# Gate and up projections of a decoder layer by Strassen's seven block products, on one core

## The chip, the core and the metric

One core of a Trainium2 chip runs the whole layer in one launch. The metric is device time in microseconds (us) of that core. TensorE (PE) multiplies, ScalarE (ACT) and VectorE (DVE) copy, split and add, GpSimd (POOL) does elementwise work too, and SyncE (SP) issues the loads.

## What is computed

The part that the change touches is the first half of the feed-forward block (512 tokens, width 1024, hidden width 2816):

```
h = rms_norm(x, ffn_norm[l])
g = jnp.einsum('bsd,df->bsf', h, w_gate[l])
u = jnp.einsum('bsd,df->bsf', h, w_up[l])
x = x + jnp.einsum('bsf,fd->bsd', jax.nn.silu(g) * u, w_down[l])
```

Ahead of it lie the attention part (two groups of heads, one input projection) and the output projection; both stay as they are.

## The kernel before

Every float32 operand of a product is split in two parts of a shorter type: a high part, which ACT copies (`ffn_hi`, L389 through `split_hi`), and a low part, which DVE gets as operand minus high part (`split_lo`, L723). `product` (L1075 to L1079) then issues three matmuls for each 128x128 tile of stationary operand: high by high, high by low, low by high.

Weights come in tiles of 128x1024 (512 KB): of the gate and the up matrix each tile holds 128 hidden columns over the whole width of 1024 (eight blocks of 128), and 22 + 22 such tiles stand in turn, gate, up, gate, up (`columns`). A ring of four slots holds the raw tile, its high and its low part. `hidden` takes one tile: 8 blocks times 3 matmuls with 512 tokens as moving operand (`H2`), into one bank of PSUM. The first four tiles are done in two passes of 256 tokens, since the last two of the four groups of 128 tokens are normed and transposed (`turn_h2`) between them. ACT takes silu of the gate bank (L667), DVE multiplies it with the up bank (`gate`, L1042), and the two split the result (L671, L1046). Then come 22 tiles of the down projection (`down`), each 24 matmuls of 512 columns, with hidden tokens as stationary operand.

All order is written by hand: each engine runs its own list, and semaphores join them. DVE has, at the entry of the stage, for each group of 128 tokens the residual add (L1011), the Newton steps of the norm (L704 to L716), the norm itself (`h_normed`, L1028) and the low part of the transposed activations (`h2_lo`, L1016). GpSimd has nothing to do after the attention part (L354 to L366 are its rotary products there, 512 elements in each of 128 partitions, both inputs in SBUF).

## Time and profile before

| what | value |
|---|---|
| time, median of 3 runs (lowest to highest) | 684.35 us (684.1 to 685.02) |
| span of the profiled execution | 685.7 us, 1.35 above the median of the runs |
| PE busy | 654.8 us, 95% of the span |
| DVE, ACT, POOL busy | 366.3, 247.9, 79.3 us |
| first matmul of gate and up | 314.94 us from the start |
| first matmul of the down projection | 559.16 us |
| last matmul | 682.12 us |

The records give no time of the profiled execution other than its span. Times in the rows count from the start of that span. The duration of a matmul in a row holds its passage through the array; successive matmuls overlap, so their pace is read from the starts.

### The profile page before, as it was taken

How to read it: one execution, taken by the hardware profiler on the slowest of the kernel's cores; microseconds unless marked ns; L12 is line 12 of the kernel's file. 1: busy time of each engine (PE TensorE's matmuls, PEld its weight loads, DVE VectorE, ACT ScalarE, POOL GpSimd, SP SyncE). 2: the span in 40 equal slices, each digit the busy share in tenths (PEclk: the TensorE clock that was granted, in tenths of full speed). 3: DMA queues.
4: the chain of work that ended last, by engine and by line, in shares of the span. 5: the costliest groups of instructions: out<-in, count | busy, mean ns of one | idle time of the engine just before them, and what ended most of it. 6: DMA issues, size and time to landing. Idle time of an engine off the chain costs nothing.

```text
span 685.7 us, 9568 instructions
## 1 busy us (share of the span) xinstructions
PE 654.8 (95%) x3220; PEld 533.4 (78%) x3220; DVE 366.3 (53%) x703; ACT 247.9 (36%) x458; POOL 79.3 (12%) x64
## 2 busy tenths in 40 slices
...
DMA packets 19944, 61.42 MB, mean 90 GB/s; under 512 B 3024, under 2 KB 3408, under 8 KB 19920
## 3 DMA queue, kind: packets, MB, share of 16 engines
...
q8 instruction: 15, 0.25, 0.2%
...
## 4 chain that ended last, share of the span: by engine, by line
PE 77%; DVE 14%; issue 4%; ACT 2%; DMA 1%; SPq 0%; DVEq 0%; ACTq 0%
PE ps L1077 24%; PE ps L1079 23%; PE ps L1078 23%; PE ps L1142 3%; DVE small L713 2%; PE ps L1157 2%; DVE small L716 1%; DVE small L788 1%; DVE small L714 1%; PE ps L1109 1%; DVE w_lo L723 1%; ACT probs L480 1%; DMA w_raw<-wt 1%; DVE probsT_lo L822 1%; PE ps L1117 1%
## 5 line engine op out<-in xcount | busy, mean ns | idle before, releaser
L1077 PE MATMUL ps<-h_parts,w_hi 128*128 128x512 f32 (+1 forms) x576 | 227.5, 395 | 3.0 <-DVE h_parts L859 2.8
L1079 PE MATMUL ps<-h_parts,w_lo 128*128 128x512 f32 (+1 forms) x576 | 220.8, 383 | 0.0
L1078 PE MATMUL ps<-h_parts,w_hi 128*128 128x512 f32 (+1 forms) x576 | 219.0, 380 | 0.0
L723 DVE TENSOR_TENSOR w_lo<-w_raw,w_hi 128x1024 fp32r<-128x1024 f32 x93 | 118.4, 1273 | 79.1 <-ACT w_hi L389 78.8
L1077 PEld LDWEIGHTS ps<-h_parts,w_hi 128*128 128x128 f32 x576 | 109.5, 190 | 26.0 <-issue 7.3
L389 ACT ACTIVATE w_hi<-w_raw 128x1024 fp32r<-128x1024 f32 x93 | 97.4, 1053 | 81.8 <-PE ps L1079 80.4
L1079 PEld LDWEIGHTS ps<-h_parts,w_lo 128*128 128x128 f32 x576 | 109.1, 189 | 22.6
L1078 PEld LDWEIGHTS ps<-h_parts,w_hi 128*128 128x128 f32 x576 | 109.5, 190 | 19.0
L1042 DVE TENSOR_TENSOR gated<-ps,silu_gate 128x512 f32<-128x512 f32 x22 | 15.2, 692 | 154.9 <-PE ps L1079 154.9
L1079 PE MATMUL ps<-w_hi,hidden_parts 128*128 128x512 f32 x176 | 69.3, 394 | 0.0
L1077 PE MATMUL ps<-w_hi,hidden_parts 128*128 128x512 f32 x176 | 69.3, 394 | 0.0
L1078 PE MATMUL ps<-w_lo,hidden_parts 128*128 128x512 f32 x176 | 69.3, 394 | 0.0
L480 ACT ACTIVATE probs<-ps,small 128x128 f32<-128x128 f32 (+3 forms) x64 | 39.0, 614 | 40.6 <-DVE small L791 40.5
L671 ACT ACTIVATE hidden_parts<-gated 128x512 f32 (+1 forms) x22 | 13.9, 633 | 100.3 <-DVE gated L1042 100.3
L1078 PEld LDWEIGHTS ps<-w_lo,hidden_parts 128*128 128x128 f32 x176 | 32.9, 187 | 8.2
L1079 PEld LDWEIGHTS ps<-w_hi,hidden_parts 128*128 128x128 f32 x176 | 32.9, 187 | 8.2
L1077 PEld LDWEIGHTS ps<-w_hi,hidden_parts 128*128 128x128 f32 x176 | 32.9, 187 | 8.1
L667 ACT ACTIVATE silu_gate<-ps 128x512 f32<-128x512 f32 x22 | 13.2, 598 | 64.8 <-PE ps L1079 64.8
L490 ACT ACTIVATE probsT_hi<-ps 128x128 fp32r<-128x128 f32 (+3 forms) x48 | 19.3, 439 | 26.4 <-PE ps L1157 26.0
L788 DVE TENSOR_REDUCE small<-ps 128x2 f32<-128x256 f32 (+3 forms) x32 | 26.4, 824 | 1.1
L362 POOL TENSOR_TENSOR q_roped<-q_gained,cos 128x512 f32<-128x512 f32 x8 | 11.0, 1372 | 127.1 <-ACT q_gained L429 127.1
L822 DVE TENSOR_TENSOR probsT_lo<-ps,probsT_hi 128x128 fp32r<-128x128 f32 (+3 forms) x48 | 21.5, 482 | 3.2 <-ACT probsT_hi L490 3.2
...
## 6 DMA issues: line engine op xcount, KB each, us to landing
w_raw<-wt SPq DMA_DIRECT2D x98, 512.0 KB, 3.4
residual<-x SPq DMA_DIRECT2D x4, 512.0 KB, 4.8
...
ffn_gain<-gain SPq DMA_DIRECT2D x1, 512.0 KB, 3.3
...
```

What stands on the lines that cost most here:

```text
L389: nc.scalar.activation(WH[:, slot], RAW[:, slot], ACT.Copy).then_inc(w_hi, 1)
L480: nc.scalar.activation(PR[qt % 2][:, a, 0:W], ps[:, 2 + a, 0:W], ACT.Exp, bias=NB[:, i:i + 1], scale=RQ[:, i:i + 1], accum_out=SUM[:, i:i ...
L490: nc.scalar.activation(PTH[:, a, 0:qt + 1, qt * P:(qt + 1) * P], ps[:, bank, 0:(qt + 1) * P].rearrange("p (k q) -> p k q", q=P), ACT.Copy) ...
L671: nc.scalar.activation(HID[:, f, 0], AC[:, par], ACT.Copy).then_inc(ah_s, 1)
L723: nc.vector.tensor_tensor(WL[:, slot], RAW[:, slot], WH[:, slot].bitcast(F32), ALU.subtract).then_inc(w_lo, 1)
L788: nc.vector.tensor_reduce(MX[:, i], ps[:, 2:4, 0:W], AX.X, ALU.max).then_inc(mx_s, 1)
L822: nc.vector.tensor_tensor(PTL[at], ps[:, bank, 0:(qt + 1) * P].rearrange("p (k q) -> p k q", q=P), PTH[at].bitcast(F32), ALU.subtract).the ...
L1042: nc.vector.tensor_tensor(AC[:, par], ps[:, 5 + 2 * par], SG[:, par], ALU.mult).then_inc(gated_s, 1)
L1077: nc.tensor.matmul(dst, lh, rh, start=start, stop=False, skip_group_check=True)
L1078: nc.tensor.matmul(dst, lh, rl, start=False, stop=False, skip_group_check=True)
L1079: return nc.tensor.matmul(dst, ll, rh, start=False, stop=stop, skip_group_check=True)
L1142: ins = nc.tensor.matmul(ps[:, 2 + a, 0:W], left[rows[a], qs], right[rows[a], 0:W], start=n == 0, stop=n == 2, skip_group_check=True)
```

## The change

The gate and up projections are cut in 11 units of 256 hidden columns (two tiles of gate, two of up). In a unit the activations are a 2x2 block matrix, first and second half of the tokens by first and second half of the width of 1024, and the weights are one too: first and second half of the width by gate (B11, B21) and up (B12, B22). Seven block products (Q1 to Q7, in Winograd's form) take the place of eight. One product is two tiles of 128 hidden columns times 4 blocks of the width times 3 matmuls: 24 matmuls with 256 tokens as moving operand. In the table of order `ORDER` a unit has seven of them, 77 in all.

- PE: `hidden` is replaced by `gate_product`. Q1, Q6, Q7 and Q4 of a unit add up in one bank, Q2, Q5 and Q3 in others; Q2 and the pair Q5/Q3 have one bank each for all units.
- GpSimd: `w_sum` makes four sums of raw weights per unit (128x1024 each): T1 = B11 + B12 (for Q5), T2 = T1 + B22 (Q6), B22 + B12 (Q7), T2 + B21 (Q4). In the first unit two sums of activations (`SR[:, 2]` and `SR[:, 3]`, also 128x1024) stand between them.
- ACT: a high part for each of the 77 products (`product_hi`), copies of the bank's partial sums (`keep_q1`, `keep_q16`, `keep_q167`), silu of both halves, and five high parts of activation sums (`sum_hi`). `product_hi(n)` waits for the product before the fourth slot came round: product n - 4.
- DVE: the 77 low parts (`product_lo`), two sums of activations in two pieces (`sums`), their five low parts (`sum_lo`), and per unit `gate_first`, `up_second`, `hidden_second` and the two operations of `up_and_hidden_first`.
- SP: loads of 512 KB as before, in another cut and into two rings of four slots; those of the second unit wait for the end of the output projection.
- The splitting of the hidden activations moves into the down stage (`hidden_hi`, `hidden_lo`), whose matmuls stay.

```diff
 LOADS_BEFORE = (RING3 // 3 + 1, RING3 // 3 + 1, RING3 // 3 + 1, 2)
 assert RING3 % 4 == 3
+def gate_order():
+    order = [(q, u) for q in ("Q1", "Q2") for u in (0,)] + [("Q1", 1), ("Q2", 1)]
+    order += [("Q6", 0), ("Q5", 0), ("Q7", 0), ("Q6", 1), ("Q4", 0), ("Q3", 0), ("Q7", 1), ("Q5", 1)]
+    for u in range(2, UNITS):
...
+            def w_sum(u, n):
+                b11, b21, b12, b22 = (unit_raw(u, role) for role in ROLES)
+                if n == 1:
+                    if u == 0:
+                        pool.wait_ge(wo_s, 2 * TT)
+                    else:
+                        pool.wait_ge(c_lo, PLACE["Q5", u - 1] + 1)
+                    unit_raw_wait(pool, u, "B11")
+                    unit_raw_wait(pool, u, "B12")
+                    nc.gpsimd.tensor_tensor(T1[:], b11, b12, ALU.add).then_inc(sums_w, 1)
+                if n == 2:
+                    if u >= 1:
+                        pool.wait_ge(c_lo, PLACE["Q6", u - 1] + 1)
+                    unit_raw_wait(pool, u, "B22")
+                    pool.wait_ge(sums_w, 4 * u + 1)
+                    nc.gpsimd.tensor_tensor(T2[:], T1[:], b22, ALU.add).then_inc(sums_w, 1)
+                if n == 3:
+                    pool.wait_ge(sums_w, 4 * u + 2)
+                    nc.gpsimd.tensor_tensor(b12, b22, b12, ALU.add).then_inc(sums_w, 1)
+                if n == 4:
+                    unit_raw_wait(pool, u, "B21")
+                    pool.wait_ge(c_lo, PLACE["Q2", u] + 1)
+                    pool.wait_ge(sums_w, 4 * u + 3)
+                    nc.gpsimd.tensor_tensor(b21, T2[:], b21, ALU.add).then_inc(sums_w, 1)
+            w_sum(0, 1)
+            w_sum(0, 2)
+            pool.wait_ge(h2r_s, TT)
+            nc.gpsimd.tensor_tensor(SR[:, 2], H2R[:, 0:KTH, 0:HALF], H2R[:, 0:KTH, HALF:SEQ], ALU.subtract).then_inc(ss3_s, 1)
+            w_sum(0, 3)
+            pool.wait_ge(ss2_s, 2)
+            nc.gpsimd.tensor_tensor(SR[:, 3], H2R[:, KTH:KT, 0:HALF], SR[:, 1], ALU.add).then_inc(ss4_s, 1)
+            w_sum(0, 4)
+            for u in range(1, UNITS):
+                for n in (1, 2, 3, 4):
+                    w_sum(u, n)
...
-            def ffn_hi(r, n):
-
-                if isinstance(r, int) and r == 0:
+            def product_hi(n):
+                if n < SLOTS:
                     act.wait_ge(wo_s, TT)
                 else:
-                    act.wait_ge(w_used, round_w_used(r - 1, n))
-                split_hi(n, r + (LOADS_BEFORE[n] + 1))
+                    act.wait_ge(c_used, n - SLOTS + 1)
+                if n >= PRODUCTS:
+                    down_raw_wait(act, n - PRODUCTS)
+                else:
+                    q, u = ORDER[n]
+                    if q in ("Q1", "Q2", "Q3"):
+                        unit_raw_wait(act, u, {"Q1": "B11", "Q2": "B21", "Q3": "B22"}[q])
+                    else:
+                        act.wait_ge(sums_w, 4 * u + {"Q5": 1, "Q6": 2, "Q7": 3, "Q4": 4}[q])
+                nc.scalar.activation(WH[:, n % SLOTS], product_source(n), ACT.Copy).then_inc(c_hi, 1)
...
+            sum_hi(0, SR[:, 1], ss2_s, 2)
+            sum_hi(1, SR[:, 0], sa_s, 2)
+            def keep_q1(u):
+                act.wait_ge(c_used, PLACE["Q1", u] + 1)
+                if u >= 1:
+                    act.wait_ge(g0_s, u)
+                nc.scalar.activation(C1[:], ps[:, bank("Q1", u)], ACT.Copy).then_inc(c1_s, 1)
...
+            def silu_first(u):
+                act.wait_ge(g0_s, u + 1)
+                nc.scalar.activation(G0[:], G0[:], ACT.Silu).then_inc(sg0_s, 1)
+            def silu_second(u):
+                act.wait_ge(c_used, PLACE["Q4", u] + 1)
+                if u >= 1:
+                    act.wait_ge(hid_s, 2 * u - 1)
+                nc.scalar.activation(G1[:], ps[:, bank("Q4", u)], ACT.Silu).then_inc(sg1_s, 1)
...
+            for n, (q, u) in enumerate(ORDER):
+                if q == "Q1":
+                    keep_q1(u)
+                if q == "Q6":
+                    keep_q16(u)
+                if q == "Q7":
+                    keep_q167(u)
+                if q == "Q4":
+                    silu_second(u)
+                if q == "Q3" and u + 1 < UNITS:
+                    silu_first(u + 1)
+                if (q, u) == ("Q2", 0):
+                    silu_first(0)
+                product_hi(n + 3)
+                if n == 1:
+                    sum_hi(2, SR[:, 2], ss3_s, 1)
+                    sum_hi(3, H2R[:, KTH:KT, HALF:SEQ], h2r_s, TT)
+                if n == 4:
+                    sum_hi(4, SR[:, 3], ss4_s, 1)
+                if n >= PRODUCTS - 2:
+                    hidden_hi(n - (PRODUCTS - 2))
+            for f in range(2, FT):
+                hidden_hi(f)
+                if f + 1 < FT:
+                    product_hi(PRODUCTS + f + 1)
...
-            def ffn_lo(r, n):
-                split_lo(n, r * 4 + (G_FFN + n + 1))
+            def product_lo(n):
+                dve.wait_ge(c_hi, n + 1)
+                nc.vector.tensor_tensor(WL[:, n % SLOTS], product_source(n), WH[:, n % SLOTS].bitcast(F32),
+                                        ALU.subtract).then_inc(c_lo, 1)
...
+            def sums(tt):
+                dve.wait_ge(h2r_s, tt + 1)
+                first, second = slice((tt - 2) * P, (tt - 1) * P), slice(tt * P, (tt + 1) * P)
+                nc.vector.tensor_tensor(SR[:, 0, :, first], H2R[:, 0:KTH, second], H2R[:, KTH:KT, second],
+                                        ALU.subtract).then_inc(sa_s, 1)
+                dve.wait_ge(sa_s, tt - 1)
+                nc.vector.tensor_tensor(SR[:, 1, :, first], SR[:, 0, :, first], H2R[:, 0:KTH, first],
+                                        ALU.subtract).then_inc(ss2_s, 1)
+            def sum_lo(i, source):
+                dve.wait_ge(sc_hi, i + 1)
+                nc.vector.tensor_tensor(SC[:, i, 1], source, SC[:, i, 0].bitcast(F32), ALU.subtract).then_inc(sc_lo, 1)
...
-                if tt >= 1:
-                    ffn_lo(0, tt - 1)
+                if tt in (1, 2):
+                    product_lo(tt - 1)
...
-                if tt >= 1:
-                    h2_lo(tt - 1)
-            ffn_lo(0, TT - 1)
-            h2_lo(TT - 1)
...
+                if tt in (1, 2):
+                    first_lo(tt - 1)
+            sums(2)
+            product_lo(2)
+            sums(3)
+            sum_lo(0, SR[:, 1])
+            sum_lo(1, SR[:, 0])
+            def gate_first(u):
+                dve.wait_ge(c1_s, u + 1)
+                dve.wait_ge(c_used, PLACE["Q2", u] + 1)
+                if u >= 1:
+                    dve.wait_ge(hid_s, 2 * u)
+                nc.vector.tensor_tensor(G0[:], ps[:, bank("Q2", u)], C1[:], ALU.add).then_inc(g0_s, 1)
...
+            def up_and_hidden_first(u):
+                dve.wait_ge(v2_s, u + 1)
+                dve.wait_ge(c_used, PLACE["Q3", u] + 1)
+                nc.vector.tensor_tensor(U0[:], ps[:, bank("Q3", u)], V2[u % 2][:], ALU.subtract).then_inc(u0_s, 1)
+                dve.wait_ge(sg0_s, u + 1)
+                dve.wait_ge(u0_s, u + 1)
+                nc.vector.tensor_tensor(HID[:, 2 * u:2 * u + 2, 0:HALF], G0[:].rearrange("p (f q) -> p f q", f=2),
+                                        U0[:].rearrange("p (f q) -> p f q", f=2), ALU.mult).then_inc(hid_s, 1)
...
+            for n, (q, u) in enumerate(ORDER):
+                if (q, u) == ("Q2", 0):
+                    gate_first(0)
+                if q == ("Q5" if u == 1 else "Q7"):
+                    up_second(u)
+                if q == "Q4":
+                    hidden_second(u)
+                if q == "Q3":
+                    up_and_hidden_first(u)
+                    if u + 1 < UNITS:
+                        gate_first(u + 1)
+                product_lo(n + 3)
+                if n == 1:
+                    sum_lo(2, SR[:, 2])
+                    sum_lo(3, H2R[:, KTH:KT, HALF:SEQ])
+                if n == 4:
+                    sum_lo(4, SR[:, 3])
+                if n >= PRODUCTS - 2:
+                    hidden_lo(n - (PRODUCTS - 2))
+            for f in range(2, FT):
+                hidden_lo(f)
+                if f + 1 < FT:
+                    product_lo(PRODUCTS + f + 1)
...
+            def gate_product(n):
+                q, u = ORDER[n]
                 if n == 0:
-                    turn_h2(2)
-                if n == 2:
-                    turn_h2(3)
-            pe.wait_ge(h2l, TT)
-            for f, j in ((0, 0), (0, 1), (1, 0), (1, 1)):
-                hidden(f, f, j, slice(SEQ // 2, SEQ))
-            with pe.Fori(1, GATE_ROUNDS) as r:
-                for par in range(2):
-                    hidden(r * 2 + par, par, 0, slice(0, SEQ))
-                    hidden(r * 2 + par, par, 1, slice(0, SEQ))
-
+                    pe.wait_ge(a1_lo, 2)
+                if u == 0 and q in ("Q6", "Q5", "Q7", "Q4", "Q3"):
+                    pe.wait_ge(sc_lo, {"Q6": 1, "Q5": 2, "Q7": 3, "Q4": 4, "Q3": 5}[q])
+                if q == "Q1":
+                    if u < 2:
+                        pe.wait_ge(res, TT + 2 * u + 1)
+                    else:
+                        pe.wait_ge(sg1_s, u - 1)
+                if q == "Q2":
+                    if u == 0:
+                        pe.wait_ge(res, TT + 2)
+                    else:
+                        pe.wait_ge(g0_s, u)
+                if q == "Q6":
+                    pe.wait_ge(c1_s, u + 1)
+                if q == "Q7":
+                    pe.wait_ge(v2_s, u + 1)
+                if q == "Q4":
+                    pe.wait_ge(v3_s, u + 1)
+                if q == "Q5" and u >= 1:
+                    pe.wait_ge(u0_s, u)
+                if q == "Q3":
+                    pe.wait_ge(u1_s, u + 1)
+                pe.wait_ge(c_lo, n + 1)
+                for f in range(2):
+                    for k in range(KTH):
+                        w = slice((f * KTH + k) * P, (f * KTH + k + 1) * P)
+                        if q in ("Q1", "Q2"):
+                            kk = k + KTH * (q == "Q2")
+                            rh, rl = A1[:, 0, kk], A1[:, 1, kk]
+                        else:
+                            i = ("Q6", "Q5", "Q7", "Q4", "Q3").index(q)
+                            rh, rl = SC[:, i, 0, k], SC[:, i, 1, k]
+                        ins = product(ps[:, bank(q, u), f * HALF:(f + 1) * HALF], WH[:, n % SLOTS, w],
+                                      WL[:, n % SLOTS, w], rh, rl,
+                                      q in ("Q1", "Q2", "Q5") and f == 0 and k == 0, k == KTH - 1)
+                ins.then_inc(c_used, 1)
...
+            gate_product(0)
+            turn_h2(2)
+            gate_product(1)
+            turn_h2(3)
+            for n in range(2, PRODUCTS):
+                gate_product(n)
             TAIL = 3
             for f in range(FT - TAIL):
-                pe.wait_ge(w_lo, G_DOWN + f + 1)
-                pe.wait_ge(al_s, f + 1)
```

What GpSimd runs after the attention part, in the changed kernel (w_sum_78 is T1, w_sum_82 is T2, h_sums are the sums of activations; before, nothing stood there):

```order
L502 TENSOR_TENSOR w_sum_78<-w_raw 128x1024 [waits raw_in2,raw_in0,out_rows]
L508 TENSOR_TENSOR w_sum_82<-w_sum_78,w_raw 128x1024 [waits w_sums_ready,raw_in3]
L521 TENSOR_TENSOR h_sums<-h_by_dim 128x1024 [waits h2_evacuated]
L511 TENSOR_TENSOR w_raw<-w_raw 128x1024 [waits w_sums_ready]
L524 TENSOR_TENSOR h_sums<-h_by_dim,h_sums 128x1024 [waits h2_sum_2]
L516 TENSOR_TENSOR w_raw<-w_sum_82,w_raw 128x1024 [waits w_sums_ready,product_lo_ready,raw_in1]
L502 TENSOR_TENSOR w_sum_78<-w_raw_odd 128x1024 [waits raw_odd_in2,raw_odd_in0,product_lo_ready]
```

Six operations of 128x1024 stand in one queue ahead of the first sum for the second unit.

What DVE runs between the norm of the last 128 tokens and the release of the bank of Q2, before the change:

```order
L1028 SCALAR_TENSOR_TENSOR h_normed<-residual,small,ffn_gain 128x1024 [waits h2_newton_step]
L1016 TENSOR_TENSOR h_parts<-ps,h_parts 128x8x128 [waits h2_hi_ready]
L723 TENSOR_TENSOR w_lo<-w_raw,w_hi 128x1024 [waits w_hi_ready]
L1016 TENSOR_TENSOR h_parts<-ps,h_parts 128x8x128 [waits h2_hi_ready]
L1042 TENSOR_TENSOR gated<-ps,silu_gate 128x512 [waits w_used,silu_ready]
```

and in the changed kernel:

```order
L1259 SCALAR_TENSOR_TENSOR h_normed<-residual,small,ffn_gain 128x1024 [waits h2_newton_step]
L1239 TENSOR_TENSOR h_sums<-h_by_dim 128x4x128 [waits h2_evacuated]
L1242 TENSOR_TENSOR h_sums<-h_sums,h_by_dim 128x4x128 [waits h2_sum_a]
L954 TENSOR_TENSOR w_lo<-w_raw_odd,w_hi 128x1024 [waits product_hi_ready]
L1239 TENSOR_TENSOR h_sums<-h_by_dim 128x4x128 [waits h2_evacuated]
L1242 TENSOR_TENSOR h_sums<-h_sums,h_by_dim 128x4x128 [waits h2_sum_a]
L1248 TENSOR_TENSOR h_sum_parts<-h_sums,h_sum_parts 128x1024 [waits h2_sum_hi_ready] x2
L954 TENSOR_TENSOR w_lo<-w_raw_odd,w_hi 128x1024 [waits product_hi_ready]
L1275 TENSOR_TENSOR gate_first<-ps,q_kept 128x512 [waits product_done,q1_kept]
L954 TENSOR_TENSOR w_lo<-w_sum_82,w_hi 128x1024 [waits product_hi_ready]
```

Five operations with both inputs in SBUF now stand behind the last evacuation of activations and ahead of `gate_first`, for which the fourth product (Q2 of the second unit) waits.

A later unit on DVE, from the low part of Q5 (w_sum_78) to that of the next product:

```order
L954 TENSOR_TENSOR w_lo<-w_sum_78,w_hi 128x1024 [waits product_hi_ready]
L1296 TENSOR_TENSOR up_first<-ps,q_kept_67 128x512 [waits product_done,q16_kept]
L1299 TENSOR_TENSOR hidden<-gate_first,up_first 128x2x256 [waits up_first_sum,silu_first]
L1275 TENSOR_TENSOR gate_first<-ps,q_kept 128x512 [waits hidden_half,product_done,q1_kept]
L954 TENSOR_TENSOR w_lo<-w_raw_odd,w_hi 128x1024 [waits product_hi_ready]
```

The first of these rows gives T1 free, and with it GpSimd's first sum of the next unit; before, the queue held only `gate`, `hidden_lo` and the low parts of weights.

## Rows read from the trace of the kernel before

**Rows 1.** Cores: span and mean granted clock of TensorE.
```profile
core 0: 685.7 us, clock 0.983
```
**Rows 2.** Windows: stretch, length, busy (instructions) of PE, PEld, DVE, ACT, POOL; PEclk, DMA.
```profile
314.90:559.20 244.30, 244.26 (x1169) 204.81 (x1170) 84.89 (x102) 72.70 (x92) 0.00 (x0) 1.00 0.28 95
...
342.00:560.00 218.00, 218.00 (x954) 178.88 (x953) 71.23 (x80) 61.01 (x78) 0.00 (x0) 1.00 0.29 96
...
319.50:342.00 22.50, 22.50 (x183) 22.04 (x183) 10.19 (x11) 9.04 (x11) 0.00 (x0) 1.00 0.22 72
```
**Rows 3.** Waits, 342 to 560 us: us in total, times, longest.
```profile
DVE gated L1042 <- PE ps L1079: 146.5, 20, 7.5
```
**Rows 4.** Timeline of PE: start us, us; first gate, first down and last matmul.
```profile
314.94 0.39 PE L1077 MATMUL ps<-h_parts,w_hi 128*128 128x256 f32 x1 [0.16 <-DVE h_parts L1016]
...
559.16 0.39 PE L1077 MATMUL ps<-w_hi,hidden_parts 128*128 128x512 f32 x1
...
682.12 0.40 PE L1079 MATMUL ps<-w_hi,hidden_parts 128*128 128x512 f32 x1
```
**Rows 5.** Timeline of PE, matmuls of 256 tokens, first and last of 54.
```profile
325.40 0.28 PE L1078 MATMUL ps<-h_parts,w_hi 128*128 128x256 f32 x1
...
331.64 0.28 PE L1077 MATMUL ps<-h_parts,w_hi 128*128 128x256 f32 x1
```
**Rows 6.** Timeline of PE, one group of transposes.
```profile
317.88 1.03 PE L1409 MATMUL ps<-ident,h_normed 128*128 128x128 f32 x8
318.67 0.36 PE L1077 MATMUL ps<-h_parts,w_hi 128*128 128x256 f32 x1
```
**Rows 7.** Groups by line and form, 345 to 555 us: count | busy us, mean ns.
```profile
L723 DVE TENSOR_TENSOR w_lo<-w_raw,w_hi 128x1024 fp32r<-128x1024 f32 x38 | 46.4, 1220 | 0.3
L389 ACT ACTIVATE w_hi<-w_raw 128x1024 fp32r<-128x1024 f32 x39 | 40.9, 1049 | 0.0
...
L667 ACT ACTIVATE silu_gate<-ps 128x512 f32<-128x512 f32 x20 | 12.0, 598 | 61.0 <-PE ps L1079 61.0
```
**Rows 8.** Timeline of DVE at the stage's entry.
```profile
313.67 1.22 DVE L1016 TENSOR_TENSOR h_parts<-ps,h_parts 128x1024 fp32r<-128x1024 f32 x1
314.82 0.69 DVE L1011 TENSOR_TENSOR residual<-ps,residual 128x512 f32<-128x512 f32 x1
...
319.03 1.28 DVE L1028 SCALAR_TENSOR_TENSOR h_normed<-residual,small,ffn_gain 128x1024 f32<-128x1024 f32 x1
```
**Rows 9.** A line of POOL: duration ns min/median/max, and two of its operations in the timeline.
```profile
L362 POOL TENSOR_TENSOR k_roped<-k_gained,cos x8: 1270/1283/2352, 29.7 to 246.2; 128x512 f32<-128x512 f32 x8
...
53.02 1.29 POOL L364 TENSOR_TENSOR q_rotated<-q_rotated,sin 128x512 f32<-128x512 f32 x1 [3.75 <-DMA q_rotated<-q_gained]
...
54.39 1.29 POOL L366 TENSOR_TENSOR q_roped<-q_roped,q_rotated 128x512 f32<-128x512 f32 x1
```
**Rows 10.** Timeline of POOL and DVE, where DVE comes second.
```profile
246.19 1.28 POOL L362 TENSOR_TENSOR k_roped<-k_gained,cos 128x512 f32<-128x512 f32 x1
246.29 2.26 DVE L723 TENSOR_TENSOR w_lo<-w_raw,w_hi 128x1024 fp32r<-128x1024 f32 x1
247.49 2.22 POOL L364 TENSOR_TENSOR k_rotated<-k_rotated,sin 128x512 f32<-128x512 f32 x1
```
**Rows 11.** Timeline of POOL and DVE, where POOL comes second.
```profile
21.89 1.22 DVE L723 TENSOR_TENSOR w_lo<-w_raw,w_hi 128x1024 fp32r<-128x1024 f32 x1
22.29 1.96 POOL L362 TENSOR_TENSOR q_roped<-q_gained,cos 128x512 f32<-128x512 f32 x1 [20.49 <-ACT q_gained L429]
23.02 1.31 DVE L876 TENSOR_TENSOR lambda_in<-lambda_in 128x64 f32<-128x64 f32 x1
```
**Rows 12.** Windows of a stretch in which PE idles and of the next.
```profile
188.00:192.00 4.00, 2.60 (x13) 2.60 (x13) 2.59 (x8) 0.72 (x2) 0.37 (x1) 0.61 0.00 0
192.00:196.00 4.00, 4.00 (x17) 2.74 (x16) 3.23 (x6) 1.65 (x3) 0.00 (x0) 0.53 0.00 0
```
**Rows 13.** DMA issues: count, KB each, median us to landing.
```profile
w_raw<-wt SPq DMA_DIRECT2D x98, 512.0 KB, 3.4
```

More of the change, by code:

```diff
@@ L67 @@
 TILES = G_DOWN + FT
-ROUNDS = (TILES - G_FFN) // 4
-REST = (TILES - G_FFN) % 4
-GATE_ROUNDS = (G_DOWN - G_FFN) // 4
-assert G_FFN % 4 == 0 and G_DOWN % 4 == 0
+UNITS = FT // 2
+HALF = SEQ // 2
+KTH = KT // 2
+SLOTS = 4
+assert FT % 2 == 0
 assert SEQ // BLOCK == 2, "MoBA is causal attention for two blocks only"
@@ L126, in build @@
         MIX, r1 = place("mixed_parts", [P, KT, 2, SEQ], F32R)
-        HID, _ = place("hidden_parts", [P, FT, 2, SEQ], F32R, r0)
+        SC, _ = place("h2_sum_parts", [P, 5, 2, KTH, HALF], F32R, r0)
+        AR, _ = place("hidden_parts", [P, SLOTS, 2, SEQ], F32R, r0)
+        RAW1, _ = place("w_raw_odd", [P, 4, D], F32, r0 + 40 * KB)
+        T1, _ = place("w_sum_1", [P, D], F32, r0 + 56 * KB)
+        V2B, _ = place("q16_kept_1", [P, SEQ], F32, r0 + 60 * KB)
+        HID, _ = place("hidden", [P, FT, SEQ], F32, r0 + 62 * KB)
+        A1, _ = place("h2_first_parts", [P, 2, KT, HALF], F32R, r0 + 106 * KB)
+        T2, _ = place("w_sum_2", [P, D], F32, at_cos)
+        V2 = (V2A, V2B)
         r2 = r1 + 32 * KB
@@ L684, in _, with sum_hi @@
-            with act.Fori(GATE_ROUNDS + 1, ROUNDS) as r:
-                for n in range(4):
-                    ffn_hi(r, n)
-            for n in range(REST):
-                ffn_hi(ROUNDS, n)
+                    h2_raw(tt - 1)
+                    if tt - 1 < 2:
+                        first_hi(tt - 1)
+            product_hi(2)
+            h2_raw(TT - 1)
+            def sum_hi(i, source, ready, n):
+                act.wait_ge(ready, n)
+                nc.scalar.activation(SC[:, i, 0], source, ACT.Copy).then_inc(sc_hi, 1)
@@ L1057, in _ @@
-            hidden_round(0)
-            with dve.Fori(1, GATE_ROUNDS) as r:
-                hidden_round(r)
-            with dve.Fori(GATE_ROUNDS + 1, ROUNDS) as r:
-                for n in range(4):
-                    ffn_lo(r, n)
-            for n in range(REST):
-                ffn_lo(ROUNDS, n)
+            for n, (q, u) in enumerate(ORDER):
[17 more added lines that the diff above has]
+                    hidden_lo(n - (PRODUCTS - 2))
```

222 lines of the change are left out of this document (144 added, 78 removed).

## The prediction

> **What bounds the kernel now.** The span is 685.7 us [rows 1], 1.35 above the median of the runs, so I forecast a difference and lay it on 684.35. The windows come first: in the 244.3 us of the gate and up stage PE is busy all the time, DVE for 84.9 us, ACT for 72.7, GpSimd not at all [rows 2]. The chain of waits agrees: DVE waits 146.5 us for PE's sums [rows 3]. So PE sets the end, and fewer columns through it are worth their whole time as long as nobody is late for it. The first gate matmul starts at 314.94, the first of the down projection at 559.16, the last of all at 682.12 [rows 4]. Only the first of these distances, 244.2 us, changes: the 528 matmuls behind 559.16 stay as they are (their 123 us), and so does what follows the last.
>
> **What PE gains.** 1056 matmuls of 512 tokens (128 of them done as pairs of 256) become 77 x 24 = 1848 of 256. The pace of the short form is in the trace: 53 steps in 331.64 - 325.40 = 6.24 us, 0.1177 each [rows 5], with fresh weights for every one; the long form has 218.0 / 954 = 0.2285 [rows 2]. Half the columns take 51.5% of the time, so the eighth saved in columns is 10% in time. A product takes 24 x 0.1177 = 2.83 us, the 77 take 217.5, and the two groups of transposes among them 2 x 0.79 [rows 6]: 219.1. The gain, if PE never waits, is 244.2 - 219.1 = **25.1 us**. In the stretch of short matmuls the weight loads are busy 22.04 of 22.5 us [rows 2]: they leave nothing over, so an error here is one towards longer; I take -1 to +4 us on the total.
>
> **What the other engines get, per unit of 19.8 us.** ACT: seven high parts of 1.05 and five operations of 0.60 [rows 7] are 10.4. DVE: seven low parts of 1.22 [rows 7] and five operations of 0.69 [rows 8] are 12.0. GpSimd: four sums of 1024 elements. The trace has only 512 elements, 1.28 us alone [rows 9]; below, 1.28 if width cost nothing, above, twice that, 2.56, if there is no fixed part. I take 2.45, near the top, since the work is the same per element: 9.8 us. Each engine alone is well covered by PE. Loads are four of 512 KB, which land in 3.4 us [rows 13]; hidden. The splitting that moves into the down stage costs DVE 0.69 + 1.22 and ACT about 0.6 + 1.05 per tile of 5.6 us; hidden.
>
> The Trainium skill, "GPSIMD Engine Reference", section 3.1, gives 4497 ns for 2048 elements. An estimate from it and the row at 512 is 2.35 us for 1024; the start-up below would be 1 us shorter by it.
>
> **The cost: DVE and GpSimd shut each other out.** A low part takes 1.22 us, but the one that came 0.10 us behind a GpSimd product took 2.26: GpSimd ended at 247.47, DVE at 248.55. GpSimd's next operation, issued at 247.49, took 2.22 in place of 1.28, for DVE's end [rows 10]. The other way round, a GpSimd product that met a running low part took 1.96, and the tiny DVE operation queued at 23.02 behind that low part took 1.31 us, until GpSimd was done [rows 11]. So of two operations with both inputs in SBUF, one on each engine, the second is held until the first ends, and with both queues full they take turns.
>
> The rule is in the Trainium skill, "SBUF — State Buffer", section "Who interferes with whom": a DVE instruction with two SBUF inputs and a GpSimd instruction that reads SBUF exclude each other, the first to issue going first. By that rule, and the trace agrees, it speaks against this change.
>
> All four sums are of this kind, and so are DVE's seven low parts (1.15 from start to start [rows 8]) and its two hidden products (some 0.6). Per unit that is 8.05 + 1.2 + 9.8 = 19.05 of 19.8 us: the shared thing is 96% full, where each engine was half idle. It shows in two places.
>
> *At the start.* Times as in the trace of before, first product at 314.9 (one more ACT copy ahead of it lies beside DVE's Newton steps).
> - Third product: due at 314.9 + 2 x 2.83 + 2 x 0.79 = 322.2. Its low part stands behind the norm of the last tokens (ends 320.3 [rows 8]; 0.5 later by GpSimd's second sum) and two pieces of `sums` (1.4), and takes 1.2: 323.4. Stall 1.2.
> - Fourth product, Q2 of unit 1: due 326.2; it waits for `gate_first`. The last transposed tokens are out of PSUM at 322.4 + 1.05 = 323.5. Then DVE has two pieces of `sums`, two `sum_lo` and `product_lo`, 1.2 + 3 x 1.15 = 4.65 us, and GpSimd has four operations ready at the same time, 9.8 us. Taking turns both are through after 14.5, at 338.0; `gate_first` 0.69: 338.7. Stall 12.5. Without the exclusion the chain would be 1.4 + 2 x 1.05 + 0.6 + 1.05 + 1.22 + 0.69 = 7.1, and the stall 4.4.
> - Fifth and sixth: their parts are made just in time, 0.6.
> - Eighth, Q6 of unit 1: due 338.7 + 0.6 + 4 x 2.83 = 350.6. Sum T1 of unit 1 waits until T1 is free, behind `product_lo` 4, two `sum_lo` and `product_lo` 5, from 340.4 on: 345.0. Two sums, once held: 351.2. High part 1.05, low part behind the third sum (353.7) 1.1: 354.8. Stall 4.2.
> - The last `sum_lo` behind the fourth sum, and unit 2 as unit 1 with less left over: 2 and 2, my estimate from one sum of 2.45 each, less cover.
>
> Sum **22.5**. After 12.5 us of idling TensorE would be at its lower clock (in the window of 188 to 192 us PE was busy 2.6 of 4 us and the mean clock 0.61 of full, then 0.53, so mostly 1.2 GHz [rows 12]). A product at half the pace costs 2.8 more; the eighth product's wait does not hang on PE and swallows one of two; I take 0, and up to 3 for the range.
>
> *In each later unit.* After Q3 the chain is up 0.69, hidden 0.69, `gate_first` 0.69, silu 0.60, high part 1.05, low part 1.22, some 0.3 of handing over: 5.2 us, for Q7 two products later, 5.66. The margin is 0.4. If the hidden product (both inputs in SBUF) meets a sum, up to 2.45 are added: stall 0 to 2. The meeting is close: T1's sum starts when the low part of Q5 is done, which from the end of Q4 is 0.2 + 0.5 + 1.05 + 1.15 + 1.22 + 0.1 = 4.2, and ends at 6.7; the hidden product falls due at 5.66 + 0.2 + 0.69 = 6.6. GpSimd needs about 0.1 between dependent operations [rows 9], and DVE slips in there. If sums took under 2.3 the second one would already run. I take 0.5 per unit, nine units: **4.5**, with 0 and 18 as ends.
>
> *At the end.* The last Q4 and the first down tile follow their producers with no product between: 0.9 each, **1.7**.
>
> Sum: -25.1 + 22.5 + 4.5 + 1.7 = +3.6; 684.35 + 3.6 = **688**.
>
> **Rivals.**
> - As above, with the hidden product slipping in: 683 to 692. Chance 0.50.
> - The hidden product is shut out in every unit, 1.5 more or so in nine: +13, 697 (692 to 702). For it: the margin is a tenth of a microsecond. Chance 0.25.
> - Faster, one mechanism: the turns at the start are not taken. GpSimd's four operations come late or DVE keeps its place when its queue is full; then the fourth product waits 4.4, not 12.5, and the eighth's wait shrinks by half: 22.5 - 8 - 2 = 12.5, time 684.35 - 6.4 = 678 (668 to 683). It decides below 19 us of start. Against it the row at 23.02, where GpSimd got its turn between two queued DVE operations [rows 11]. With no exclusion at all, about 672. Chance 0.23.
> - The short matmul is slower in a long run than in 54, since loads of weights fill all its time: each 0.005 us is 9 us, 697. Against it: 0.1177 without a break in the trace. Chance 0.02.
>
> A measurement of this kernel tells 0.2% (1.4 us) from no change. Faster 0.24, same 0.12 (of the first case, 683 to 685.7), slower 0.64. Range 676 to 699; the likeliest case's own is 683 to 692.
>
> **What will show it.** Matmuls of 256 at a pace of 0.118, 2.83 per product. POOL sums of 2.3 to 2.6 alone and up to 3.7 when held; low parts of up to 3.6 between 323 and 338. PE idle some 12 us ahead of the fourth product, released by DVE `gate_first`, and 4 ahead of the eighth; a lower clock behind the first. Later idle spots once per unit, at Q7, under 0.5 us (1.5 to 2 in the second case), with a long DVE `hidden`. I am wrong if low parts beside sums stay at 1.2 us, if PE's idle time in the stage is under 20 us, or if the pace of the products is not 2.83.

## The result

The changed kernel takes 715.53 us (median of 4 runs, 714.15 to 716.68), the kernel before 684.66 beside it: ratio 1.0442, 95% interval 1.0413 to 1.0471. It is slower, as forecast, but by 31 us where 3.6 were forecast, and outside the range.

The windows of the changed kernel, in the form of [rows 2] (stretch, length, busy time of PE, PEld, DVE, ACT, POOL with instructions, granted clock, DMA); the last is the down projection:

```profile
span 714.8 us, 10764 instructions
...
313.80:337.90 24.10, 10.97 (x89) 10.36 (x89) 21.20 (x23) 8.91 (x11) 15.45 (x6) 0.83 0.30 109
337.90:385.00 47.10, 40.32 (x303) 39.80 (x304) 31.43 (x24) 21.87 (x27) 21.48 (x9) 0.91 0.26 90
385.00:588.10 203.10, 186.09 (x1475) 184.12 (x1474) 127.40 (x108) 85.37 (x109) 80.66 (x32) 0.94 0.28 94
588.10:711.30 123.20, 123.17 (x528) 98.66 (x528) 43.03 (x50) 30.45 (x40) 0.00 (x0) 1.00 0.20 70
```

The down projection takes the same time as before: 711.17 - 588.13 = 123.0 us from its first matmul to its last, and 682.12 - 559.16 = 123.0 before. All of the difference is in the gate and up stage: 588.13 - 313.80 = 274.3 us against 244.2 [rows 4]. Where PE runs without a break the pace is as predicted: 57 steps between these two rows, 6.72 us, 0.1179 each.

```profile
384.80 0.28 PE L1344 MATMUL ps<-h_sum_parts,w_hi 128*128 128x256 f32 x1
...
391.52 0.28 PE L1344 MATMUL ps<-h_sum_parts,w_hi 128*128 128x256 f32 x1
```

So the work is close to the predicted 219.1 us, and 274.3 - 219.1 = 55.2 are something else. The rows of PE's timeline with an idle time in brackets give most of it:

```profile
321.33 1.09 PE L1675 MATMUL ps<-ident,h_normed 128*128 128x128 f32 x8 [0.73 <-DVE h_normed L1259]
323.88 0.36 PE L1343 MATMUL ps<-h_first_parts,w_hi 128*128 128x256 f32 x1 [1.46 <-DVE w_lo L954]
337.88 0.58 PE L1343 MATMUL ps<-h_first_parts,w_hi 128*128 128x256 f32 x1 [10.94 <-DVE gate_first L1275]
353.80 0.36 PE L1343 MATMUL ps<-h_sum_parts,w_hi 128*128 128x256 f32 x1 [2.00 <-DVE w_lo L954]
358.29 0.36 PE L1343 MATMUL ps<-h_sum_parts,w_hi 128*128 128x256 f32 x1 [1.43 <-DVE w_lo L954]
373.19 0.35 PE L1343 MATMUL ps<-h_first_parts,w_hi 128*128 128x256 f32 x1 [3.36 <-DVE w_lo L954]
...
464.38 0.36 PE L1343 MATMUL ps<-h_sum_parts,w_hi 128*128 128x256 f32 x1 [1.93 <-DVE w_lo L954]
486.37 0.43 PE L1343 MATMUL ps<-h_sum_parts,w_hi 128*128 128x256 f32 x1 [1.96 <-DVE w_lo L954]
...
581.45 0.38 PE L1343 MATMUL ps<-h_sum_parts,w_hi 128*128 128x256 f32 x1 [0.69 <-ACT q_kept L854]
588.13 0.47 PE L1343 MATMUL ps<-w_hi,hidden_parts 128*128 128x512 f32 x1 [0.77 <-DVE hidden_parts L1305]
```

The start stands for 19.9 us, the eight stalls ahead of Q7 (393.88 to 556.86, one per unit from unit 2 to unit 9) for 15.6, the end for 1.5: together 37.0.

The other 18.2 us have three parts. A bracket counts from the end of the last matmul, 0.28 us behind its start, while in unbroken work the next one starts 0.118 behind it. So each of the 16 stalls costs 0.16 more than its bracket (0.30 for the one behind the transposes); call it the restart: 2.7 us. Work at a lower granted clock is the largest part. Behind the two longest stalls, and behind the one at 486.37, the windows show it, while behind the one at 464.38 the clock did not fall:

```profile
338.00:340.00 2.00, 2.00 (x10) 2.00 (x11) 0.54 (x1) 2.00 (x3) 0.00 (x0) 0.50 0.00 0
...
374.00:376.00 2.00, 2.00 (x12) 2.00 (x11) 1.91 (x3) 0.00 (x0) 0.00 (x0) 0.50 0.32 71
...
486.00:488.00 2.00, 1.63 (x8) 1.66 (x9) 2.00 (x3) 0.00 (x0) 0.00 (x0) 0.63 0.00 0
488.00:490.00 2.00, 2.00 (x12) 2.00 (x11) 0.49 (x1) 0.00 (x0) 0.00 (x0) 0.52 0.21 32
490.00:492.00 2.00, 2.00 (x19) 2.00 (x19) 0.37 (x1) 1.00 (x2) 0.00 (x0) 1.00 1.00 379
...
464.00:466.00 2.00, 1.62 (x14) 1.65 (x15) 2.00 (x3) 0.00 (x0) 0.00 (x0) 1.00 0.00 0
```

From the stall at 464.38 to the next are 21.99 us, 19.9 of work and 2.1 of waiting; between the others 23.5 (486.37 to 509.85, for one). So a stall of 1.95 us cost another 1.5 in lower clock, seven times of eight: 10.5 us. At the start the steps between matmuls are longer behind 337.88 (2.4 us in all) and behind 373.19 (1.5): 3.9. The remaining 1.1 us are the pace, which in a whole unit is a little longer than in the prediction (19.9 us, not 24 x 7 x 0.1177 = 19.8).

What makes Q7 late is in the timelines of DVE and POOL in one unit:

```profile
478.86 0.69 DVE L1296 TENSOR_TENSOR up_first<-ps,q_kept 128x512 f32<-128x512 f32 x1 [1.78 <-PE ps L1345]
479.65 0.69 DVE L1299 TENSOR_TENSOR hidden<-gate_first,up_first 128x512 f32<-128x512 f32 x1
480.48 0.69 DVE L1275 TENSOR_TENSOR gate_first<-ps,q_kept 128x512 f32<-128x512 f32 x1
482.82 3.40 DVE L954 TENSOR_TENSOR w_lo<-w_raw,w_hi 128x1024 fp32r<-128x1024 f32 x1 [1.65 <-ACT w_hi L572]
...
477.15 2.40 POOL L502 TENSOR_TENSOR w_sum<-w_raw_odd 128x1024 f32<-128x1024 f32 x1 [4.32 <-DVE w_lo L954]
479.72 2.95 POOL L508 TENSOR_TENSOR w_sum<-w_sum,w_raw_odd 128x1024 f32<-128x1024 f32 x1 [0.17 <-POOL w_sum L502]
482.75 2.39 POOL L511 TENSOR_TENSOR w_raw_odd<-w_raw_odd 128x1024 f32<-128x1024 f32 x1
```

The hidden product (479.65) slips in between two sums, as the prediction assumed: it keeps its 0.69 us, and the second sum (479.72) takes 2.95 for it. But the low part that Q7 needs becomes ready at 482.82, 0.07 us after the third sum started at 482.75, and takes 3.40 us instead of 1.22. It is done at 486.22, and Q7 starts at 486.37.

### The profile page after: what moved, and what is told of

Its sections match the earlier page's. It is cut to its first block, busy times and chain, and to the rows that moved or that the text cites. A ratio compares the mean times of both kernels' runs of the same rounds, so it can differ in the third digit from the quotient of the medians.

```text
span 714.8 us, 10764 instructions
## 1 busy us (share of the span) xinstructions
PE 644.7 (90%) x3916; PEld 560.4 (78%) x3916; DVE 473.7 (66%) x776; ACT 302.5 (42%) x531; POOL 198.2 (28%) x110
## 4 chain that ended last, share of the span: by engine, by line
PE 59%; DVE 27%; issue 6%; ACT 5%; DMA 1%; POOL 1%; SPq 0%; DVEq 0%; ACTq 0%; POOLq 0%
PE ps L1343 18%; PE ps L1345 17%; PE ps L1344 17%; DVE w_lo L954 6%; PE ps L1408 2%; ACT w_hi L572 2%; DVE small L927 2%; DVE small L926 2%; DVE w_lo L936 1%; DVE small L1004 1%; PE ps L1423 1%; DVE small L929 1%; ACT probs L635 1%; DVE h_sum_parts L1248 1%; DVE probsT_lo L1038 1%
## 5 line engine op out<-in xcount | busy, mean ns | idle before, releaser
L1343 PE MATMUL ps<-h_sum_parts,w_hi 128*128 128x256 f32 x440 | 128.5, 292 | 19.7 <-DVE w_lo L954 19.0
L1344 PE MATMUL ps<-h_sum_parts,w_hi 128*128 128x256 f32 x440 | 127.9, 291 | 0.0
L1345 PE MATMUL ps<-h_sum_parts,w_lo 128*128 128x256 f32 x440 | 127.6, 290 | 0.0
L1343 PEld LDWEIGHTS ps<-h_sum_parts,w_hi 128*128 128x128 f32 x440 | 87.3, 199 | 21.8 <-issue 20.9
L954 DVE TENSOR_TENSOR w_lo<-w_raw_odd,w_hi 128x1024 fp32r<-128x1024 f32 x37 | 56.8, 1536 | 48.3 <-ACT w_hi L572 48.3
L1345 PEld LDWEIGHTS ps<-h_sum_parts,w_lo 128*128 128x128 f32 x440 | 87.8, 200 | 0.0
L1344 PEld LDWEIGHTS ps<-h_sum_parts,w_hi 128*128 128x128 f32 x440 | 87.6, 199 | 0.0
L1343 PE MATMUL ps<-h_parts,w_hi 128*128 128x512 f32 x192 | 82.0, 427 | 3.1 <-DVE h_parts L1075 3.1
L1345 PE MATMUL ps<-h_parts,w_lo 128*128 128x512 f32 x192 | 76.4, 398 | 0.0
L1344 PE MATMUL ps<-h_parts,w_hi 128*128 128x512 f32 x192 | 75.9, 395 | 0.0
L1343 PE MATMUL ps<-h_first_parts,w_hi 128*128 128x256 f32 x176 | 51.7, 294 | 16.1 <-DVE gate_first L1275 10.9
L572 ACT ACTIVATE w_hi<-w_raw 128x1024 fp32r<-128x1024 f32 x40 | 41.9, 1050 | 40.1 <-PE ps L1345 40.1
L1344 PE MATMUL ps<-h_first_parts,w_hi 128*128 128x256 f32 x176 | 51.2, 291 | 0.0
L1343 PEld LDWEIGHTS ps<-h_parts,w_hi 128*128 128x128 f32 x192 | 36.8, 192 | 13.7 <-issue 7.7
```

The costliest lines, as they stand in the source:

```text
L572: nc.scalar.activation(WH[:, n % SLOTS], product_source(n), ACT.Copy).then_inc(c_hi, 1)
L954: nc.vector.tensor_tensor(WL[:, n % SLOTS], product_source(n), WH[:, n % SLOTS].bitcast(F32), ALU.subtract).then_inc(c_lo, 1)
L1343: nc.tensor.matmul(dst, lh, rh, start=start, stop=False, skip_group_check=True)
L1344: nc.tensor.matmul(dst, lh, rl, start=False, stop=False, skip_group_check=True)
L1345: return nc.tensor.matmul(dst, ll, rh, start=False, stop=stop, skip_group_check=True)
```

## The experiments

The median of the kernel before was 684.86 us beside the first four experiments and 685.85 beside the other four. Since the start of the stage shifts by a few us from profile to profile, the stage itself (first gate matmul to first down matmul) is compared too.

**The third sum held.** GpSimd's third sum from unit 2 on waits until the low part of the previous unit's Q7 is done.

```diff
                 if n == 3:
+                    if u >= 2:
+                        pool.wait_ge(c_lo, PLACE["Q7", u - 1] + 1)
                     pool.wait_ge(sums_w, 4 * u + 2)
```

> GpSimd's third sum of each unit from the third on waits until the low part of Q7 of the unit before is made; nothing else moves. Exclusion theory (a DVE operation with two SBUF inputs is held by a running GpSimd sum): the low part of Q7, 3.4 us in the changed kernel, is 1.2 again, PE's stall of 1.95 us per unit and the lower clock behind it (23.49 us per unit against 21.99 in the one unit without the drop and 19.8 of work) go in eight units: 8 x 3.7 = 30 us less, 686; up to 695 if the sum then meets another low part with less cover than I think. Rival, GpSimd's sums themselves come too late for PE: holding one longer makes no difference or costs, 715 or more. Rival, DVE and ACT are too slow for the chain without any meeting: 715.

Measured: 693.88 us (692.12 to 696.26), ratio 1.0138 (1.0091 to 1.0186), 21.7 us less than the changed kernel and inside the 686 to 695 that were expected. The stage takes 563.71 - 311.15 = 252.6 us. The timelines of DVE, POOL and PE at the same place:

```profile
469.68 1.22 DVE L956 TENSOR_TENSOR w_lo<-w_raw,w_hi 128x1024 fp32r<-128x1024 f32 x1 [1.65 <-ACT w_hi L574]
471.11 3.37 DVE L956 TENSOR_TENSOR w_lo<-w_raw_odd,w_hi 128x1024 fp32r<-128x1024 f32 x1 [0.20 <-ACT w_hi L574]
...
470.99 2.41 POOL L513 TENSOR_TENSOR w_raw_odd<-w_raw_odd 128x1024 f32<-128x1024 f32 x1 [1.45 <-DVE w_lo L956]
...
474.63 0.36 PE L1345 MATMUL ps<-h_first_parts,w_hi 128*128 128x256 f32 x1 [0.51 <-DVE w_lo L956]
```

The low part of Q7 now takes 1.22. The sum catches the next one, that of Q1 of the unit after, by 0.12 us, and PE waits 0.51 us there instead of 1.95; the unit is 20.56 us. The operations and their number are the same, and a low part of 3.4 us stands in each unit as before, one product later: a start moved by one operation is worth 21.7 us. That settles which meeting costs the time in the later units.

**TensorE kept busy.** 16 matmuls of 256 columns into a bank whose contents nobody uses, ahead of Q7's waits, from unit 2 on (nine units, 1.88 us each at the pace above); nothing else changes, the low part comes as late as before.

```diff
                 if q == "Q7":
+                    if u >= 2:
+                        for i in range(16):
+                            nc.tensor.matmul(ps[:, 2, 0:HALF], SC[:, 1, 0, 0, 0:P], SC[:, 1, 0, 0], start=True, stop=True,
+                                             skip_group_check=True)
                     pe.wait_ge(v2_s, u + 1)
```

> Ahead of Q7's waits PE gets 16 extra matmuls of 256 columns into a bank that nobody reads (16 x 0.118 = 1.9 us), from the third unit on; the output is unchanged. If the 1.5 us between units of 23.49 and of 21.99 is the lower clock after PE's 1.95 us of idling, the granted clock stays at 1.00 in all later units, their period is 22.0, and 8 x 1.5 = 12 us go: 703. Rival, the clock falls for another reason or costs nothing: 715, or 717 with the extra matmuls not wholly inside the idle time.

Measured: 707.99 us (705.44 to 710.66), ratio 1.0333 (1.0278 to 1.0388), 7.5 less than the changed kernel.

```profile
385.00:560.00 175.00, 174.34 (x1471) 172.94 (x1470) 117.28 (x96) 76.38 (x96) 80.92 (x32) 1.00 0.28 95
```

The clock stays at 1.00 from 385 to 560 us, and a unit takes 21.99 us (496.16 to 518.15 between two DVE `up_first`; one unit took 21.44), the length of the one unit of the changed kernel in which the clock had not fallen. The time is above the 703 expected, for two reasons. The expectation counted eight losses of 1.5, and the clock had fallen only seven times; and the last unit had no stall to fill, so its 1.88 us come on top. Seven times 1.5 less 1.88 is 8.6; the stage shrank by 274.3 - (579.68 - 312.95) = 7.6. Of the 1.0 between them the window above has 0.7 as idle time that the extra matmuls did not fill (PE is busy 174.34 of 175 us). So the lower clock is a cost of its own beside the waiting.

**Sums of 8 columns.** Unit 0 has its first two sums in full; its other two, and all sums of units 1 to 10, cover 8 of 1024 columns.

> Leaves out nearly all of the weight sums: from the second unit on each covers 8 of 1024 columns, in the first unit T1 and T2 stay whole; so Q5, Q6, Q7 and Q4 are not the reference's. All waits and the two activation sums stay. Exclusion theory: every stall after the first 25 us of the stage goes (3.7 x 8, and the 2.0, 1.4 and 3.4 of the first units), and the 10.9 of the fourth product loses two of its four turns (5): about 715.5 - 29.6 - 6.8 - 5 - 2 (clock) = 672. Rival, the chain on DVE and ACT behind Q3 is too long by itself: a stall at each Q7 stays, 700 or more.

Measured: 675.94 us (one run); the stage takes 547.51 - 314.45 = 233.1. The only stalls left:

```profile
321.98 1.09 PE L1676 MATMUL ps<-ident,h_normed 128*128 128x128 f32 x8 [0.73 <-DVE h_normed L1260]
324.53 0.37 PE L1344 MATMUL ps<-h_first_parts,w_hi 128*128 128x256 f32 x1 [1.46 <-DVE w_lo L955]
334.37 0.58 PE L1344 MATMUL ps<-h_first_parts,w_hi 128*128 128x256 f32 x1 [5.25 <-DVE gate_first L1276]
540.93 0.39 PE L1344 MATMUL ps<-h_sum_parts,w_hi 128*128 128x256 f32 x1 [0.69 <-ACT q_kept L855]
547.51 0.47 PE L1344 MATMUL ps<-w_hi,hidden_parts 128*128 128x512 f32 x1 [0.87 <-DVE hidden_parts L1306]
```

Without the sums nothing is late in units 2 to 10, and of the 10.94 us at the start 5.7 go. The new chains on ACT and DVE (kept products, first gate half) are covered. The stalls add up to 9.0 us; 233.1 - 219.1 - 9.0 = 5.0 are left. By the steps between matmuls 0.9 of them is the cost of five restarts, some 3 are lower clock (0.50 from 326 to 328 us and from 334 to 338), and the rest is the pace. The 672 expected had 2 for the clock.

**The sums replaced by writes.** Each sum is two `memset` of the same 1024 columns: as many instructions in the same place, twice, but without SBUF inputs, and with values that are not the sums.

> Each of the 44 weight sums is replaced by two memsets of the same tile, so GpSimd writes 128x1024 and reads nothing, about 1.0 us each and 2 us together (the sums are constants, so the output is not the reference's). If only GpSimd operations that read SBUF shut out a DVE operation with two SBUF inputs: low parts of 1.2 us, no stall at Q7, 672 as without sums. If any GpSimd operation on SBUF does: low parts of up to 3.3 us beside memsets, 695 or more.

Measured: 674.42 us (one run); the stage takes 546.03 - 313.05 = 233.0, as with sums of 8 columns. POOL and DVE side by side:

```profile
454.54 0.96 POOL L518 MEMSET w_raw_odd<- 128x1024 f32 x1
...
455.08 1.23 DVE L963 TENSOR_TENSOR w_lo<-w_raw,w_hi 128x1024 fp32r<-128x1024 f32 x1 [1.65 <-ACT w_hi L581]
```

A low part that starts during a `memset` keeps its 1.23 us, and so do all others of the stage (1.21 to 1.23, and 2.36 for two in a row). GpSimd being busy, writing the same columns, holds nobody; an operation that also reads does. The Trainium skill says this in "SBUF — State Buffer", section "Who interferes with whom": DVE with two SBUF inputs contends with a GpSimd instruction that reads SBUF, not with one that only writes. This run agrees. (At the start 8.54 us stand ahead of Q2 of unit 1 and not 5.25 as in the run before; the third product had come earlier, and Q2 of unit 1 itself starts 19.6 us behind the first matmul here and 19.9 there.)

**The sums on DVE.** Units 1 to 10 get their four sums from DVE, placed in its list where their inputs are done; GpSimd keeps the four of unit 0 and the two token sums.

```diff
-            for u in range(1, UNITS):
-                for n in (1, 2, 3, 4):
-                    w_sum(u, n)
...
+            SUM_AT = {}
+            for u in range(1, UNITS):
+                steps = (3 if u == 1 else PLACE["Q6", u] - 5, PLACE["Q6", u] - 4, PLACE["Q7", u] - 4, PLACE["Q4", u] - 4)
+                for i, at in enumerate(steps):
+                    SUM_AT.setdefault(at, []).append((u, i + 1))
...
                 product_lo(n + 3)
...
+                for which in SUM_AT.get(n, ()):
+                    w_sum(*which)
```

> The forty weight sums of units 1 to 10 are issued by VectorE, between its low parts, and GpSimd does only the four of unit 0 and its two token sums; the arithmetic is the same. Theory (the time lost behind the start comes from the two engines excluding each other, not from the amount of work): VectorE's work in a unit becomes 7 x 1.22 + 4 x 0.69 + 4 x 1.22 = 16.2 us of 19.8, nothing holds the low part of Q7, the period is 19.8 us instead of 23.5, and the clock stays at full speed. The start keeps its 10.9 us of idle time. Worked out from the run that held the third sum: 693.9, less 9 x (20.56 - 19.8) = 6.8, less the 2.5, 1.4 and 3.4 us that it still stood in units 0 and 1, gives 681 us (679 to 685), faster than the kernel before. Rival (VectorE is simply overloaded in a unit, and any more work on it makes it the bound): stalls at Q7 or Q4 of over 1 us in each unit and 700 us or more.

Measured: 681.03 us (678.06 to 683.6, 9 runs), ratio 0.9942 (0.9916 to 0.9968): 0.6% less than the kernel before, a small gain, but a ratio of 1 lies outside the interval. The 681 expected was met. The stage takes 554.43 - 315.31 = 239.1. The window of the later units:

```profile
385.00:560.00 175.00, 173.55 (x1440) 171.74 (x1440) 141.28 (x143) 85.44 (x107) 0.00 (x0) 1.00 0.33 115
```

Two groups of DVE in it, a low part and a sum (count, busy us, mean ns, idle time before them):

```profile
L951 DVE TENSOR_TENSOR w_lo<-w_raw_odd,w_hi 128x1024 fp32r<-128x1024 f32 x24 | 29.3, 1222 | 12.4 <-ACT w_hi L569 12.4
L1318 DVE TENSOR_TENSOR w_sum<-w_sum,w_raw 128x1024 f32<-128x1024 f32 x4 | 4.9, 1220 | 0.0
```

All of PE's stalls from Q2 of unit 1 to the last product:

```profile
339.39 0.58 PE L1371 MATMUL ps<-h_first_parts,w_hi 128*128 128x256 f32 x1 [9.40 <-DVE gate_first L1272]
369.92 0.36 PE L1371 MATMUL ps<-h_sum_parts,w_hi 128*128 128x256 f32 x1 [0.48 <-DVE w_lo L951]
384.83 0.36 PE L1371 MATMUL ps<-h_sum_parts,w_hi 128*128 128x256 f32 x1 [0.54 <-DVE w_lo L951]
547.74 0.39 PE L1371 MATMUL ps<-h_sum_parts,w_hi 128*128 128x256 f32 x1 [0.69 <-ACT q_kept L851]
```

DVE is busy 81% of the later units. It is late twice, by 0.5 us, in units 1 and 2, and not once from 385 us on: the stall at 547.74 is released by ACT. A unit takes 19.9 us (478.98 to 498.88 between two `up_first`). One sum takes it 1.22 us where GpSimd needs 2.4. The rival, that DVE would be overloaded, is out. More work on the fuller engine was 34 us faster than the same work beside it.

**The start in another order**, alone and with the sums on DVE. ACT keeps Q1 of unit 0 and DVE does the first gate half and two low parts ahead of the token sums of the last tiles. DVE's part of the edit is shown; ACT's list changes in the same way:

```diff
-            sums(2)
-            product_lo(2)
-            sums(3)
-            sum_lo(0, SR[:, 1])
-            sum_lo(1, SR[:, 0])
...
+            product_lo(2)
+            gate_first(0)
+            product_lo(3)
+            sums(2)
+            sums(3)
+            sum_lo(0, SR[:, 1])
+            product_lo(4)
+            sum_lo(1, SR[:, 0])
```

> The changed kernel with only the start in the other order (as in the run with both). Theory: the idle time moves from Q2 of unit 1 to Q6 of unit 0 at about 11 us, the stalls of 1.95 us in front of each Q7 stay, and the time stays at 715 (713 to 718). Rival (order at the start is what is lost): 705 us.

> The kernel with the sums of units 1 to 10 on VectorE, and the start in another order: ScalarE keeps Q1 of unit 0 and VectorE does the first gate half and the low parts of Q1 and Q2 of unit 1 ahead of the token sums of tiles 2 and 3. Theory (the idle time at the start is that of the whole start work, which the order can only move): the 10.9 us in front of Q2 of unit 1 shrink to about 1, and about as much appears in front of Q6 of unit 0, since that product needs the token sums; 681 us, within 2 of the kernel without the new order. Rival (the idle time comes from the first gate half standing behind the token sums alone): 671 to 675 us.

Measured alone: 713.46 us (one run); the stalls of about 2 us ahead of each Q7 stay (1.92 to 2.15). With the sums on DVE: 680.1 us (677.06 to 682.73, 10 runs), ratio 0.9919 (0.9897 to 0.994), stage 552.39 - 313.24 = 239.2 against 239.1: the order changed nothing that the runs can tell. The stall only moves, from `gate_first` to the token sums, as this row of the kernel with both shows (ahead of Q6 of unit 0):

```profile
339.17 0.55 PE L1374 MATMUL ps<-h_sum_parts,w_hi 128*128 128x256 f32 x1 [10.64 <-DVE w_lo L952]
```

**GpSimd held at the start.** With the sums on DVE, GpSimd's four operations of the start wait for the first gate half.

```diff
             pool.wait_ge(h2r_s, TT)
+            pool.wait_ge(g0_s, 1)
```

> The kernel with the sums of units 1 to 10 on VectorE, and GpSimd's four operations behind its second sum (two token sums, third and fourth weight sum of unit 0) wait until the first gate half is written. Theory: the part of the start idle that comes from exclusion, 10.9 - 5.3 = 5.6 us by the run with sums of 8 columns, leaves the gap in front of Q2 of unit 1 (5 us stand there), but the four operations of 2.4 us now come late and a gap of 5 to 7 us appears in front of Q5 or Q7 of unit 0; 681 us, within 2. Rival (they are hidden there): 675 to 677 us.

Measured: 681.19 us (678.21 to 683.23, 10 runs), ratio 0.9938 (0.9917 to 0.996); stage 549.80 - 309.92 = 239.9.

```profile
326.56 0.38 PE L1372 MATMUL ps<-h_first_parts,w_hi 128*128 128x256 f32 x1 [1.98 <-DVE gate_first L1273]
340.20 0.55 PE L1372 MATMUL ps<-h_sum_parts,w_hi 128*128 128x256 f32 x1 [6.19 <-DVE w_lo L952]
...
326.65 2.39 POOL L522 TENSOR_TENSOR h_sums<-h_by_dim 128x1024 f32<-128x1024 f32 x1 [11.96 <-DVE gate_first L1273]
329.00 3.40 POOL L511 TENSOR_TENSOR w_raw<-w_raw 128x1024 f32<-128x1024 f32 x1
332.36 3.33 POOL L525 TENSOR_TENSOR h_sums<-h_by_dim,h_sums 128x1024 f32<-128x1024 f32 x1
```

The stall ahead of Q2 of unit 1 is 1.98 us, below the 5.3 expected; but 6.19 stand ahead of a later product, where the held operations now take turns with DVE's low parts (3.40, 3.33). The stage is not shorter. In three orders the work at the entry that has to be done before the next products costs PE 8 to 11 us of waiting (9.4, 10.6, and 1.98 + 6.19 = 8.2); it can be moved, and none of the three removed it.

## Why the prediction was wrong

**The gain.** Predicted 219.1 us of PE work from 0.1177 us per matmul. Measured: 0.1179 in the changed kernel, and the seven-product unit takes 19.9 us where nothing waits (with the sums on DVE). So the gain was there, about 1 us short of the forecast. The rival of a slower short matmul is out.

**Exclusion.** Predicted from [rows 10, 11]. Right: sums take 2.35 to 2.44 us alone (2.45 predicted) and up to 3.33 held, low parts up to 3.40 held; and with writes in place of sums nothing was held.

**The start.** Predicted 22.5 us of idle time, with 12.5 ahead of the fourth product and its start at 338.7. Measured 19.9, 10.94 and 337.88. The 1.2 ahead of the third product were 0.73 + 1.46, the 4.2 ahead of Q6 of unit 1 were 2.00, and the two of 2 each behind it were 1.43 and 3.36; errors of both signs cancel in part in the sum. The faster rival (turns not taken) fell: DVE's two `sum_lo` took 5.67 us for 2.4.

**In each later unit: the step that failed.** The prediction gave it 0.5 us per unit, 4.5 in all, and it was about 27 in all: eight stalls that cost 2.1 each and seven losses of 1.5 at the lower clock. The chain it laid out (up, hidden, `gate_first`, silu, high part, low part) was the right one. Its margin of 0.4 us was nearer 0.2 (with sums of 8 columns one low part of Q7 ends at 457.77 and Q7 starts at 457.97), still enough where nothing is held. It asked at one link, the hidden product, whether a sum would be in the way, and there the answer was right too: 0.69 us at each up to the last, but for one of 2.15, at 365.08, in the first units. It did not ask at the last link, the low part, which is also of the excluding kind. At the start it had asked: there the low part of Q6 of unit 1 is put "behind the third sum". By its own numbers, counted from the end of Q4, GpSimd's second sum ends at about 9.2 us (6.7 + 2.45), or 9.8 with the hidden product let in, and GpSimd goes straight into the third, of 2.4 us; the low part falls due at about 9.6 (5.66 + 5.2 less its own 1.22). That is a near tie which had to be priced: 0.2 us decide whether a stall of 1.6 to 2 us stands in each unit. In the trace the sum came first by 0.07. The slip-in of the hidden product also made the wait longer: it put off the second sum's end by 0.6, so that the third had all of its time still ahead when the low part came (this is argued from the timeline, no run tried it). The second case, 697 us, had a stall of about the right size from the wrong meeting, and its sum is off: 1.5 us more in nine units is 13.5 on top of 688, so 701. Holding the third sum (693.88) showed the meeting, and moving the sums away (681.03) the size.

**The clock after idle time, taken as 0.** The prediction looked at it only behind the 12.5 us of the start. There it was 2.4, inside the 0 to 3 allowed, and 1.5 more behind the stall at 373.19; in the later units, where it was not looked at, 10.5. The run with PE kept busy isolated the latter. A stall of 1.95 us thus cost 3.6 us (23.5 - 19.9).

**The end.** Predicted 1.7, measured 0.69 + 0.77 = 1.5.

By the forecast's own terms, with what it had no term for at the end: -25.1 + 19.9 + 15.6 + 1.5 + 2.7 (restarts) + 3.9 + 10.5 (lower clock) + 1.1 (pace) = +30.1, the measured difference of the stages (274.3 - 244.2).

What stays open: why the clock did not fall after one of eight equal stalls, and how much of the entry's 8 to 11 us another scheme for the first products could save, which no run tried. The clock varies like this elsewhere too: with only the start in another order it stayed at 1.00 behind two of the eight stalls (439.86 and 507.81 us), and behind the 1.46 us ahead of the third product it stayed at 1.00 in the changed kernel (324 to 326) and fell to 0.50 with the sums on DVE (326 to 328), where the stall that follows is 9.40 and not 10.94 us. The 5 us gained by the sums on DVE leave 20 of the 25.1 unused: 14.1 are idle time (0.73, 1.46, 9.40 at the start, 0.5 twice, 1.5 at the end), 1.2 restarts, about 3 lower clock and the rest the pace.
